# The last oct's down products in six places of the banks, and the overflow block's first down product ahead of the first scatters

## What is computed

```python
def hier_moe(h, p):
    ...
    dense_w = jnp.sum(jax.nn.one_hot(flat, MOE_N_EXPERTS, dtype=F32) * top_w[..., None], 1).astype(t.dtype)
    gate = jnp.einsum('td,edf->tef', t, p['moe_w_gate'])
    up = jnp.einsum('td,edf->tef', t, p['moe_w_up'])
    hid = jax.nn.silu(gate) * up * dense_w[..., None]
    return jnp.einsum('tef,efd->td', hid, p['moe_w_down']).reshape(B, L, D)
...
    x = layer_norm(ALPHA * x + g2 * hier_moe(h, p), p['ln2_g'], p['ln2_b'])
```

## Time and profile before

| | |
|---|---|
| median of 3 runs | 1182.96 us (1179.23 to 1189.03) |
| the profiled execution | 1176.83 us, of which the span of instructions is 1175.0 us |
| TensorE busy | 1010.0 us, 86% of the span |
| VectorE busy | 554.6 us, 47% |
| ScalarE busy | 345.3 us, 29% |
| tail of layer 0, `turns` to the last scatter | about 607.8 to 637.0 us |
| tail of layer 1 | about 1127.5 to 1155.8 us |

### The profile page before, as it was taken

One profiled execution on the slowest core, in us unless ns is written; L12 is line 12 of the kernel. 1 busy time (PEld: TensorE's weight loads), 2 busy tenths in 40 slices (PEclk: granted clock), 3 DMA queues, 4 the chain that ended last, 5 costly groups with the idle time before them and its releaser, 6 DMA issues. The chain is left out here.

```text
span 1175.0 us, 19801 instructions
## 1 busy us (share of the span) xinstructions
PE 1010.0 (86%) x8162; PEld 591.6 (50%) x8162; DVE 554.6 (47%) x1239; ACT 345.3 (29%) x728; POOL 82.9 (7%) x94
## 2 busy tenths in 40 slices
PE   3788778899978999999977899789968999999982
PEld 2456557665445634535323657655454644445321
DVE  5640132478564334241576713778563343242367
ACT  2220000346132242333332211436132333333331
POOL 1110000010140000000001500000140000000000
PEclk9589979999987989899889799999978999999997
DMA  9877767850357879899993533110367779898971
GB/s 344 337 270 277 277 278 280 321 197 20 143 227 283 331 269 422 344 386 383 417 421 115 227 112 106 60 54 18 144 251 289 301 319 420 346 421 358 414 299 56
DMA packets 48670, 309.54 MB, mean 263 GB/s; under 512 B 6084, under 2 KB 6341, under 8 KB 15789
## 3 DMA queue, kind: packets, MB, share of 16 engines
q1 hardware_dynamic: 40380, 275.66, 58.7%
q0 software_dynamic: 7424, 30.27, 7.3%
q10 hardware_dynamic: 760, 2.19, 0.5%
HBM read 303.11 MB, written 4.98 MB: 262 GB/s over the span
## 5 line engine op out<-in xcount | busy, mean ns | idle before, releaser
L955 PE MATMUL bank<-sel,h_hi 128*128 128x384 f32 x192 | 83.9, 437 | 9.4 <-DVE sel L1975 9.4
L625 PE MATMUL bank<-ring,arena 128*32 128x64 f32 x3072 | 58.6, 236 | 31.9 <-DMA ring<-in_w_mod 24.0
L862 PE MATMUL bank<-ring,act_t 128*128 128x512 f32 x192 | 84.1, 595 | 0.0
L955 PEld LDWEIGHTS bank<-sel,h_hi 128*128 128x128 f32 x192 | 64.5, 336 | 29.6 <-issue 23.3
L955 PE MATMUL bank<-sel,h_lo 128*128 128x384 f32 x192 | 79.1, 412 | 0.0
L976 PE MATMUL bank<-ring,arena 128*32 128x512 f32 x480 | 62.5, 640 | 17.6 <-DVE act_t L2013 11.3
L1402 ACT ACTIVATE arena<-bank 128x384 f32<-128x384 f32 x64 | 31.4, 491 | 156.9 <-PE bank L955 156.9
L625 PEld LDWEIGHTS bank<-ring,arena 128*32 128x32 f32 x3072 | 51.7, 121 | 45.4 <-issue 21.0
L698 PE MATMUL bank<-act_t,ring 128*128 128x384 f32 x192 | 65.7, 505 | 5.1 <-DMA ring<-in_w_in 5.1
L1064 PE MATMUL bank<-y_hi,selT 128*128 128x512 f32 x144 | 62.0, 431 | 7.0 <-DVE y_lo L2036 6.7
L955 PEld LDWEIGHTS bank<-sel,h_lo 128*128 128x128 f32 x192 | 65.4, 340 | 0.0
(11 more groups left out here) (326 smaller groups left out, 1736.2 us busy)
## 6 DMA issues: line engine op xcount, KB each, us to landing
ring<-in_moe_gate_up SPq DMA_DIRECT2D x60, 1024.0 KB, 9.4
ring<-in_w_mod SPq DMA_DIRECT2D x48, 1024.0 KB, 9.4
region_k<-in_moe_gate_up SPq DMA_DIRECT2D x44, 1024.0 KB, 8.4
ring<-in_moe_down SPq DMA_DIRECT2D x32, 1024.0 KB, 9.4
arena<-in_moe_down SPq DMA_DIRECT2D x28, 1024.0 KB, 9.3
arena<-in_moe_gate_up SPq DMA_DIRECT2D x20, 1024.0 KB, 10.2
ring<-in_w_in SPq DMA_DIRECT2D x10, 1024.0 KB, 7.7
ring<-in_w_out SPq DMA_DIRECT2D x8, 1024.0 KB, 5.2
```

Of the source, the lines that this page charges most:

```text
L625: mm = pe.matmul(ps[MOD_BANK[g]][32 * j:32 * j + 32, c * 64:c * 64 + 64], cT[:, k, :], w[:, k, j * 64:j * 64 + 64], start=(k == 0), stop=( ...
L862: mm = pe.matmul(ps[2 * t + half][:, :], act_t[:, 2 * c + k, t * P:(t + 1) * P], w[:, k, half * 512:(half + 1) * 512], start=(c == 0 and k ...
L955: mm = pe.matmul(ps[gather_bank(o, k)][:, 0:TOK], src[:, t, k:D:K8], sel[:, t, :, :].rearrange("p v n -> p (v n)"), start=(t == 0 and i == ...
```

## The change

In the last oct the six products get the banks 4, 5, 0, 1, 2, 4 instead of 4 and 5 in turn; the other octs keep theirs. The wait ahead of a product is kept for i = 0 and 1, dropped for i = 2, 3 and 4, whose banks nobody in the tail uses before, and for i = 5, which uses bank 4 again, it is for the remainder of i = 0. ScalarE and VectorE read the same banks. In TensorE's list `down_over(last, 0)` moves ahead of scatter(0), `down(last, 2)` and `down(last, 3)` move ahead of scatter(2), and `down_over(last, 1)` stands between scatter(2) and scatter(3). The lists of ScalarE, VectorE and SyncE keep their order.

```diff
+def y_bank(o, i):
+
+    return (4, 5, 0, 1, 2, 4)[i] if o == OCTS - 1 else 4 + i % 2
...
-            def y_free(n):
-                if n >= 2:
+            def y_free(o, i):
+                n = BLOCKS * (OCTS * l + o) + i
+                if o < OCTS - 1 and n >= 2:
                     pe.wait_ge(e["y_low"], n - 1)
+                elif o == OCTS - 1 and i in (0, 1, BLOCKS - 1):
+                    pe.wait_ge(e["y_low"], n - 1 if i < 2 else n - 4)
...
             down(last, 0)
             choices(last, 1)
             down(last, 1)
+            down_over(last, 0)
             scatter(last, 0)
-            down_over(last, 0)
             scatter(last, 1)
-            scatter(last, 2)
             down(last, 2)
             down(last, 3)
+            scatter(last, 2)
+            down_over(last, 1)
             scatter(last, 3)
-            down_over(last, 1)
             scatter(last, 4)
             scatter(last, 5)
...
-                act.activation(y_hi[:, n % 2, :], ps[4 + n % 2][:, :], ACT.Copy, scale=column(o, i % VISITS)).then_inc(e["y_high"], 1)
+                act.activation(y_hi[:, n % 2, :], ps[y_bank(o, i)][:, :], ACT.Copy, scale=column(o, i % VISITS)).then_inc(e["y_high"], 1)
...
-                dve.scalar_tensor_tensor(y_lo[:, n % 2, :], ps[4 + n % 2][:, :], rt[:, weight:weight + 1], y_hi[:, n % 2, :].bitcast(F32),
+                dve.scalar_tensor_tensor(y_lo[:, n % 2, :], ps[y_bank(o, i)][:, :], rt[:, weight:weight + 1], y_hi[:, n % 2, :].bitcast(F32),
```

More of the change, by code:

```diff
@@ L1032, in down @@
                 c = CHUNK_AT["D", o, i]
-                n = BLOCKS * (OCTS * l + o) + VISITS * half
                 pe.wait_ge(e["hd_out"], 2 * (OCTS * l + o + 1))
@@ L1037, in down @@
                     if k == 0:
-                        y_free(n + v)
+                        y_free(o, VISITS * half + v)
                     for j in range(UNITS):
-                        mm = tile(ps[4 + (n + v) % 2], hdT[2 * v + k], weights(c)[:, 2 * j + v, :], j, k == 0, k == 1)
+                        mm = tile(ps[y_bank(o, VISITS * half + v)], hdT[2 * v + k], weights(c)[:, 2 * j + v, :], j, k == 0, k == 1)
                 mm.then_inc(e["done"], 1)
             def down_over(o, half):
-                n = BLOCKS * (OCTS * l + o) + VISITS * half + 2
-                y_free(n)
+                y_free(o, VISITS * half + 2)
                 for k in range(2):
@@ L1049, in down_over @@
                     for j in range(UNITS):
-                        mm = tile(ps[4 + n % 2], hdT[4 + k], stage[c % 2][:, j, :], j, k == 0, k == 1)
+                        mm = tile(ps[y_bank(o, VISITS * half + 2)], hdT[4 + k], stage[c % 2][:, j, :], j, k == 0, k == 1)
                     mm.then_inc(e["over"], 1)
```

## The result

The changed kernel takes 1168.26 us (median of 20 executions, 1159.65 to 1179.67) beside 1177.89 us for the kernel before (20 executions, 1165.66 to 1191.17): a ratio of 0.9923, 95% interval 0.9902 to 0.9944. It is faster, by a little less than the 1% that the prediction named; the forecast was 1177.2 us, in a range from 1170 to 1185. The ratio, like those of the experiments, leaves out executions of over 1.5% above the fastest of their kernel, so it differs a little from the quotient of the two medians (0.9918); the means further on take in all executions, and without those the differences between them change by 0.8 us at most.

The account below looks back on a forecast made before the run. The chain of waits was taken to run through y_rest(5) in both layers' tails, held up by TensorE's stalls. Gaining 2.86 us per layer, 5.72 in all, off the median 1182.96 gave 1177.2 us, range 1170 to 1185.

Parts of the forecast that it names:

- The first move: TensorE's tail: down_over(last, 0) fills the idle 1.67 us ahead of scatter(0), which stays 3.6 us after down(last, 1).
- scatter(2): TensorE's tail: scatter(2) comes 10.4 us after down(last, 1) starts, 8.8 before, with a scatter taken at 1.59 us.
- The second move: Stall of 1.66 us ahead of scatter(3) roughly halved, moved into down_over(last, 1), released by VectorE's copy: 0.7 to 1.0 us.
- y_rest(5): VectorE in each tail: 17.2 us after down(last, 1) instead of 20.07, limited by y_high(5) waiting for scatter(3); 2.86 us per layer.
- Banks: ScalarE and VectorE reading other banks in the tail: taken as nothing, as a bound 0.02 us per read, 0.2 in all.
- The sum: Both layers' tails: 2 x 2.86 = 5.72 us saved, bounds 5.1 to 6.1.
- The base: Whole kernel: the saving was taken off 1182.96 us, the median of the runs shown, giving 1177.2.
- The range: Whole kernel: 1170 to 1185 us, from the forecast with the earlier runs' spread and the cases of no gain.
- One layer only: Rival: between layer 0's tail and the projection one layer's gain is lost; gain 2.86 us, time 1180.1; chance 0.10.
- The late chunk: Rival: last chunk lands after 1144.59, new order loses, from 1145.32 on 0.73 us per layer, 1184.4; chance 0.06.
- The clock: Rival: walking through five banks lowers TensorE's clock in the tail; loss 9.1 us per layer, 1201.1 in all; chance 0.03.

Follow-up runs that it names:

- e7_copyfirst: Changed kernel with VectorE's copy of the fourth down chunk moved ahead of summed of the first half: 1171.17 us, ratio 0.9966 to the kernel before.
- e4_banks: Changed kernel's new banks alone, with TensorE's list as in the kernel before: 1175.87 us, ratio 1.0007 to the kernel before.
- e9_again: Changed kernel with no edit, timed and profiled again: 1172.81 us, ratio 0.9977 to the kernel before.
- e8_best: Changed kernel with scatter(2) ahead of down 2 and 3, and VectorE's copies, residuals and statistics moved earlier: 1168.73 us, ratio 0.9943 to the kernel before.
- e2_first: Changed kernel's banks with only down_over(last, 0) moved ahead of scatter(0), second half in the old order: 1169.47 us, ratio 0.9933 to the kernel before.
- e3_second: Changed kernel's banks with only down 2 and 3 moved ahead of scatter(2), down_over(last, 0) behind scatter(0): 1172.28 us, ratio 0.9960 to the kernel before.
- the better order: The kernel of e8_best, timed twice against the kernel before: 1168.73 us, ratio 0.9943, and 1168.40 us, ratio 0.9921.

## Why the prediction was right or wrong

**The first move: right.** scatter(0) at 3.60 us was forecast and is at 3.59, with the overflow product in the gap and no idle row.

**scatter(2): right in kind, 0.23 off.** Forecast 10.38 us after down(last, 1), measured 10.15. The scatter taken at 1.59 was one with products on both sides. Two in a row take 1.51 and 1.48 (622.94 to 624.45, and on to down(last, 2) at 625.93). The prediction had named that end of its bound (0.2 more gain) and not taken it.

**The second move: right.** The stall was to be halved and moved into down_over(last, 1), 0.7 to 1.0 us released by VectorE's copy; it is 0.73, and e7_copyfirst takes it away by moving that copy alone.

**y_rest(5): right.** 17.2 us forecast, 17.05 to 17.10 measured. The limit is, as the step said, y_high(5) waiting for scatter(3); VectorE's own list is ready 0.26 us earlier, where the forecast had the two 0.11 apart.

**Banks: right.** e4_banks changes y_rest(5) by 0.01 us per layer.

**The sum: right.** 5.72 forecast with bounds from 5.1 to 6.1; 6.0 in the traces, 5.6 ± 1.6 in all executions. What it lacks to 6.0 comes mainly from the scatters in a row, as above.

**The base: wrong, and with it the number.** The step that failed is the last one of the sum, which took the saving off 1182.96, a median of three. Twenty executions of the same kernel, these three among them, have 1177.89, and 123 have a median of 1176.81, so the base was 5 to 6 us too high, about as much as the whole gain. The profiled execution (1176.83) lay nearer to the truth, and the text said that it would lead to 1171.1; it then took the median of three. From 1177.15, the mean of all, the same sum gives 1171.4, and the changed kernel's mean is 1171.6. Of the 9.0 us between the forecast of 1177.2 and the 1168.26 measured, 5.1 are thus the base (1182.96 beside 1177.89) and 0.3 the saving (6.0 beside 5.72). The other 3.6 stand in no row; the median of all 56 executions of the changed kernel, 1171.4, lies 3.2 above that of the first twenty, so most of it did not come again.

**The range: too narrow below.** Its lower end, 1170, was the forecast with the single low execution taken into account. That leaves no room below for a base that is 5 us off and, on top of it, a comparison that strays: executions of one kernel have a standard deviation of 4.9 us, and the first twenty of the changed kernel have a mean of 1169.1, 2.4 below that of all 56.

**One layer only: it did not come.** In all profiles the projection follows `summed` by 22.2 to 22.3 us, and the end of the span follows the last `summed` by 18.9. One layer's gain alone would be 2.9 us, outside the 5.6 ± 1.6 of all executions. The stretch from the projection to layer 1's tail differs by 10 us between the profiles, so it can't be read there.

**The late chunk: it came, in one tail of eight, and cost less than the gain.** In e9_again the chunk was there 9.05 us after down(last, 1) started, 0.77 late for the new order. Before, the product wanted it only at 12.11. The prediction put the point from which the new order loses at 11.38 after the start (1144.59); that was not reached. So the price of the lost cover is real, some 0.1 us per tail on the average of eight, and the mechanism decides nothing here.

**The clock: it did not fall in the tail, but it rose late in three of 24.** In layer 1 of the profiled execution, TensorE's timeline and then the windows (busy us of PE, PEld, DVE, ACT, POOL; PEclk; DMA share; GB/s):

```profile
1137.36 3.64 PE L981 MATMUL bank<-region_k,region_w 128*32 128x512 f32 x16
...
1142.67 0.50 PE L1070 MATMUL bank<-y_hi,selT 128*128 128x512 f32 x1
```

```profile
1135.00:1139.00 4.00, 4.00 (x18) 0.90 (x14) 1.41 (x3) 0.22 (x1) 0.00 (x0) 0.50 1.00 418
1139.00:1143.00 4.00, 4.00 (x29) 1.11 (x22) 1.13 (x2) 1.27 (x2) 0.00 (x0) 0.77 0.56 231
1143.00:1159.00 16.00, 14.53 (x84) 7.40 (x82) 10.33 (x19) 5.53 (x9) 0.00 (x0) 1.00 0.01 4
```

The lower level (0.50 granted, 1.2 of 2.4 GHz) lasts into down(last, 1), which takes 3.64 us instead of 1.92; it began ahead of all that the change moved. From scatter(0) to y_rest(5) the granted clock is 1.00 in this and in every other profiled tail, through all six places of the banks. 1.71 us, the difference of scatter(0) at 5.31 and 3.60, is the whole of what layer 1's tail lacks in the table. In e7_copyfirst and e8_best the lower level lasted on into the moved overflow product, in layer 1; e8_best:

```profile
1130.29 1.72 PE L981 MATMUL bank<-small,act_t 128*32 128x512 f32 x8
```

Its first half takes 1.72 instead of 1.04 us there, and scatter(0) comes 5.93 us after down(last, 1). That is 0.62 us later than 5.31, at a place that was idle time before. So a late rise of the clock seems to cost more with the moved product in the gap; that is worked out from these two distances, as no profile of the order of before has such a tail. The Trainium skill, "TensorE: Matmul & The Clock Gate", section "A second HAM failure mode: psum-queue depth-cycling", reports a kernel in which cycling through the banks with small idle times let the clock swing; no tail profiled here shows that.

## What to carry to other kernels

Where an engine stands still for a chain of others, put work there that does not hang on that chain, and give it the storage that lets it go early; the storage alone brought nothing here. Then look what stands behind the moved piece in the other engines' lists, because a copy that sat behind a late sum became the next stall, and note which loads are now wanted earlier. Before taking a small gain off a median of a few runs, compare it with the spread of those runs: here the base was off by about as much as the gain.

## What the runs showed of the hardware

**Time goes with the mean granted clock.** Over the 230 executions of these kernels whose clock is on record, straight lines of one slope, with a level of its own for each kernel, fall by 8.6 us per 0.01 more of TensorE's mean granted clock: the changed kernel took 1159.65 us at 0.931 and 1179.46 at 0.916. With the clock taken out, the standard deviation within a kernel falls from 4.7 to 2.4 us, and the changed kernel is 6.7 ± 0.8 us below the kernel before, e2_first 5.0 ± 1.5, e3_second 2.6 ± 1.5, e4_banks 0.2 ± 1.4, e7_copyfirst 8.1 ± 1.5, the better order 7.0 ± 1.1. For five of the six the traces' 6.0, 3.7, 1.8, 0.0 and 7.8 lie within these; for the better order, 9.6 by the traces, they do not, and what is missing there stays open. Some of what this adds to the gains is by construction, since the idle time that was removed stood at a clock of 1.00 and takes the mean down with it. The changed kernel's mean clock is 0.9217, that of before 0.9231; whether that difference is chance stays open.

**Where the tile shape changes, TensorE takes longer.** A product (128 x 32 tiles) is followed by a product after 1.74 us and by a scatter (128 x 128) after 1.83 to 1.86. A scatter between two products takes 1.58 to 1.60, two scatters in a row 1.51 and 1.48, together 0.19 less than two single ones. So going over to the other shape and back costs about 0.3 us (0.1 on the product, 0.2 on the scatter); that is an estimate from these rows, and no run changes the shape alone. The Trainium skill, "TensorEngine Tiling (Array Packing)", section "Key Properties", says that changing the tiling mode drains TensorE; the 0.3 us fit that, though no row shows the drain itself.
